# State-space stage: TensorE accumulates the four products of the turned-back states in three of four units

## The reference, cut to what matters

```
def step(x, u_blk):
    bu = einsum('btgh,gph->btgp', u_blk, b_bar)          # complex
    bu = bu.at[:, 0].add(a_bar * x)
    _, xs = associative_scan(affine_compose, (a, bu))    # xs_t = a_bar xs_(t-1) + bu_t
    y = einsum('btgp,ghp->btgh', xs, c_mat).real
```

## Time and profile before

| | |
|---|---|
| time, median of 3 runs | 2393.43 us (2393.11 to 2394.8) |
| span of the profiled execution | 2391.8 us |
| TensorE busy | 2247.6 us (94%) |
| VectorE busy | 1480.2 us (62%) |
| ScalarE busy | 1084.7 us (45%) |
| granted TensorE clock, mean | 0.981 |

### The profile page before, as it was taken

One profiled execution on the slowest core, in us unless ns is written; L12 is line 12 of the kernel. 1 busy time (PEld: TensorE's weight loads), 2 busy tenths in 40 slices (PEclk: granted clock), 3 DMA queues, 4 the chain that ended last, 5 costly groups with the idle time before them and its releaser, 6 DMA issues.

```text
span 2391.8 us, 35981 instructions
## 1 busy us (share of the span) xinstructions
PE 2247.6 (94%) x15110; PEld 1802.5 (75%) x15110; DVE 1480.2 (62%) x2392; ACT 1084.7 (45%) x1834; POOL 127.0 (5%) x171
## 2 busy tenths in 40 slices
PE   7988899999999999988999989989999998769999
PEld 5755567888886777778999853357888887669999
DVE  6477547565557577866467235655566576995454
ACT  5455434232226466655456345644232334545453
POOL 0000000000000000000010011200200101000210
PEclk9999999999999999999999999999999999989999
DMA  8263453444435555434554223442443435633543
GB/s 298 73 234 113 180 211 122 154 150 142 153 138 193 163 177 169 159 132 146 177 185 143 93 71 123 159 175 87 160 153 130 159 115 195 228 127 134 212 177 124
DMA packets 180753, 372.50 MB, mean 156 GB/s; under 512 B 7664, under 2 KB 108272, under 8 KB 167280
## 3 DMA queue, kind: packets, MB, share of 16 engines
q1 hardware_dynamic: 180592, 370.21, 44.6%
HBM read 339.74 MB, written 30.44 MB: 155 GB/s over the span
## 4 chain that ended last, share of the span: by engine, by line
PE 77%; DVE 15%; ACT 5%; issue 2%; DMA 1%; SPq 1%; POOL 0%; DVEq 0%; ACTq 0%; POOLq 0%
PE ps L169 76%; DVE sb_R L200 7%; DVE sb_R L232 2%; ACT sb_R L252 1%; DVE sb_H L200 1%; PE ps L179 1%; DVE sb_R L229 1%; DVE sb_X L217 1%; SPq L263 1%; DVE sb_WP L200 1%; DMA sb_R<-mod_w 1%; ACT sb_R L258 1%; DVE sb_R L217 1%; ACT L245 0%; DVE sb_R L214 0%
## 5 line engine op out<-in xcount | busy, mean ns | idle before, releaser
L169 PE MATMUL ps<-sb_HP,sb_WP 128*128 128x512 f32 (+1 forms) x5808 | 1071.1, 345 | 11.8 <-DVE sb_HP L200 5.5
L169 PEld LDWEIGHTS ps<-sb_HP,sb_WP 128*128 128x128 f32 x5808 | 915.1, 190 | 151.6 <-issue 12.9
L200 DVE TENSOR_TENSOR sb_WP<-sb_slot,sb_WP 128x1024 fp32r<-128x1024 f32 x380 | 468.1, 1237 | 545.7 <-ACT sb_WP L258 545.0
L258 ACT ACTIVATE sb_WP<-sb_slot 128x1024 fp32r<-128x1024 f32 x380 | 399.3, 1057 | 702.9 <-PE ps L169 680.4
L169 PE MATMUL ps<-sb_XP,sb_WP 128*128 128x256 f32 (+1 forms) x2976 | 498.9, 330 | 0.6 <-DVE sb_R L200 0.4
L169 PEld LDWEIGHTS ps<-sb_XP,sb_WP 128*128 128x128 f32 x2976 | 446.4, 191 | 52.3 <-DVE sb_R L200 0.9
L200 DVE TENSOR_TENSOR sb_R<-sb_R 128x256 f32<-128x256 f32 (+4 forms) x379 | 185.4, 524 | 8.5 <-ACT sb_R L252 5.6
L169 PE MATMUL ps<-sb_R 128*32 128x64 f32 (+7 forms) x1768 | 152.8, 285 | 29.6 <-DVE sb_R L200 7.7
L169 PEld LDWEIGHTS ps<-sb_R 128*32 128x32 f32 (+3 forms) x1768 | 106.6, 151 | 66.7 <-issue 30.2
L252 ACT ACTIVATE sb_R<-ps 128x512 f32<-128x512 f32 (+1 forms) x208 | 99.9, 513 | 103.9 <-PE ps L169 99.4
L252 ACT ACTIVATE sb_R<-sb_R 128x512 f32<-128x512 f32 (+4 forms) x111 | 76.2, 689 | 79.5 <-DVE sb_R L200 78.1
(11 more groups left out here) (161 smaller groups left out, 1895.3 us busy)
## 6 DMA issues: line engine op xcount, KB each, us to landing
sb_slot<-mlp_w SPq DMA_DIRECT2D x32, 2048.0 KB, 7.9
sb_slot<-mod_w SPq DMA_DIRECT2D x12, 2048.0 KB, 7.5
sb_R<-ada_w SPq DMA_DIRECT2D x12, 2048.0 KB, 7.6
sb_slot<-ada_w SPq DMA_DIRECT2D x24, 1024.0 KB, 4.9
sb_slot<-ffn_w_gate SPq DMA_DIRECT2D x22, 1024.0 KB, 5.5
sb_slot<-ffn_w_up SPq DMA_DIRECT2D x22, 1024.0 KB, 8.0
sb_slot<-ffn_w_down SPq DMA_DIRECT2D x9, 2048.0 KB, 7.8
sb_slot<-odd_w_in SPq DMA_DIRECT2D x32, 512.0 KB, 7.6
```

What stands on the lines that cost most here:

```text
L169: return self.e.matmul(out, w, x, start=start, stop=stop, skip_group_check=True)
L200: return BLANK if self.e is None else self.e.tensor_tensor(out, a, b, op)
L258: return self.e.activation(out, a, ACT.Copy) if scale is None else self.e.activation(out, a, ACT.Copy, scale=scale)
```

## The change

In units 0, 1 and 2 VectorE no longer adds the products of the turning back. It writes four planes of 64 columns a row, two into the halves of each row of `Vi` and two into the halves of `Vr`: the product of the real parts, minus the product of the imaginary parts (one `scalar_tensor_tensor`), and the two mixed products. They can't all be written at once, since the sources lie in `Vr` and `T1`: the first half of `Vr` overlaps the source in one column, so that the third product waits for the two before it, and the fourth for the third. TensorE runs each output matmul once for each plane, so that the accumulation in PSUM makes the sums. Unit 3 stays as it was.

```
+    def halves(self, z):
+        return self.v3(z)[:, :, 0:64], self.v3(z)[:, :, 64:128]
...
+        if u < 3:
+            (re1, re2), (im1, im2) = self.halves(Vi), self.halves(Vr)
+            pr, pi, Zr, Zi = (self.read(z) for z in (pr, pi, Vr, T1))
+            e.mul(re1, pr, Zr).then_inc(*e.sig())
+            e.stt(re2, pi, -1.0, Zi, ALU.mult, ALU.mult).then_inc(*e.sig())
+            e.wait_ge()
+            e.mul(im1, pi, Zr).then_inc(*e.sig())
+            e.wait_ge()
+            e.mul(im2, pr, Zi).then_inc(*e.sig("scanned", u))
+            return
...
-        XX = [self.v3(self.V[u % 2][:, 1, :]), self.v3(self.V[u % 2][:, 0, :])]
+        parts = self.halves if u < 3 else lambda z: (self.read(z),)
+        XX = [(i, x) for i in range(2) for x in parts(self.V[u % 2][:, 1 - i, :])]
...
-                for i in range(2):
+                for n, (i, x) in enumerate(XX):
                     for j in range(4):
                         q = 4 * j + f
-                        m = e.mm(o[32 * j:32 * j + 32, s, :], self.CA[u // 3][i][s + 1][:, j, f, :], XX[i][:, q, 63:127], False, s == 3 and i == 1)
+                        m = e.mm(o[32 * j:32 * j + 32, s, :], self.CA[u // 3][i][s + 1][:, j, f, :], x[:, q, :], False, s == 3 and n == len(XX) - 1)
```

## The result

The changed kernel takes 2402.7 us in the median (2400.53 to 2405.6, four runs) against 2394.11 us (2393.11 to 2394.82, four runs): a ratio of 1.004, interval 1.0029 to 1.0052. It is slower by some 9 us; forecast were 2405.2 us. The profiled execution took 2405.6 us, its span 2403.8 us.

The account below looks back on a forecast made before the run. VectorE bounds the scans now; afterwards TensorE, with 11.3 us of slack, decides. 3X - 11.3 = 13.3 us, less 1.5 us at outputs 3, makes +11.8 us: span 2403.6 us, time 2405.2 us, range 2396 to 2414 us.

Parts of the forecast that it names:

- What bounds the kernel: Four scans: VectorE's chain runs without pause to the last sums; TensorE is a second chain with 11.3 us of slack.
- VectorE's part: Turning back in units 0 to 2: 7.0 us becomes 5.0 us, a gain of 2.0 us a unit (0.5 to 2.4).
- X: TensorE's added cost a unit, outputs 0 to 2, for 256 more records: 8.2 us, ends 6.4 to 11.0 us.
- Along the chain: Scans 2 and 3: VectorE waits for later inputs, 0.5 and 9.5 us late; outputs 3 start 13.3 us later.
- Outputs 3: Unit 3's output matmuls get cheaper by 1.5 us (0 to 3.3) at the full clock.
- The loads: CA of units 1 and 2 and matrices of unit 3 stay hidden, costed at nothing; otherwise 1.5 us a load.
- A: Rival in TensorE's outputs: extra instruction blocks come in time, X = 3.9 us; +0.9 us, 2394.3 us, no change; chance 0.11.
- B: Rival: TensorE's clock falls to 0.5 over much of outputs 0 to 2 and inputs behind; +21.7 us, 2415 us; chance 0.09.
- C: Rival: VectorE stays the bound throughout, outputs 3 start 6 us sooner, 2387 us; needs X under 1.8 us; chance 0.06.

Follow-up runs that it names:

- dve_alone: Changed kernel's VectorE products without sums in units 0 to 2, but TensorE reads one plane of two, 256 records a unit as before: 2385.87 us, ratio 0.9959 to before.
- pe_alone: Kernel before, VectorE keeping its sums, with each output matmul of units 0 to 2 issued twice on the same sums: 2403.37 us, ratio 1.0030.
- narrow: Changed kernel with the second plane's matmuls moving 8 columns and not 64, as many instructions: 2402.08 us, ratio 1.0026 to before.
- wide: Changed kernel's VectorE, but TensorE issues one matmul of 128 columns for two of 64, 256 records a unit as before: 2387.25 us, ratio 0.9969 to before.
- unit1: Kernel before with the change made in unit 1 alone: ratio 0.9996 to before.
- unit2: Kernel before with the change made in unit 2 alone: ratio 0.9994 to before.
- early: Kernel before, but in unit 3 the real sum comes first and is signalled by itself, and TensorE runs its 128 records first: ratio 0.9987 to before.

## Why the prediction was right

- **What bounds the kernel** held: TensorE's second chain with 11.3 us of slack, which dve_alone (ratio 0.9959) and pe_alone (1.0030) show from both sides.
- **VectorE's part**: 4.9 us a unit against the 5.0 us forecast. The new operation takes 1.22 us where I took 1.35 us; it costs hardly more than a product.
- **X, TensorE's part**: 8.2 us were taken. From the first to the last record, outputs 0, 1, 2 took 14.3, 14.7 and 12.0 us against 6.6, 7.6 and 5.3 us: X = 7.7, 7.1 and 6.7 us. That is 21.5 us over three units, 3.1 us under the 24.6 us forecast. Inputs 3 took 1.5 us more as well (12.6 against 11.1 us), with pauses of 0.45 and 2.74 us in place of one of 1.60 us. The prediction had that term at nothing, so it was luck that it brought half of the miss back: 23.0 us in all. The mis-sized term is X: two further blocks at the pitch of 3.47 us are 6.9 us. I had taken nearly the mean of three pauses of 1.26 to 3.56 us, two of them the first of their outputs, while the pauses between the further blocks are 0.5 to 2.0 us; that a first pause holds time in which the queue starts again is my reading and not shown.
- **Along the chain**: from outputs 0 to outputs 3 94.8 us against 82.7 us, +12.0 us, forecast 13.3. The waits of VectorE stand where they were put (scan 2 short, scan 3 over 9 us, then the ratios), and none of TensorE is left at outputs 3. The prediction looked only at the third product of scan 3; 7.49 us of the wait stand before the first two, which want the real plane of the same inputs. The end is the same: from 2058.17 us, recurrence 3 starts 77.5 us later, and 77.6 us were forecast (2134.7 - 2057.04).
- **Outputs 3**: 9.69 us became 8.32 us to the gated product, 1.4 us less against the 1.5 us forecast; a pause of 4.35 us stands where one of 2.86 us was.
- **The loads** stayed hidden: TensorE has no wait for a DMA in the stage.
- **A** (blocks in time) fell by the pauses, four in outputs 0 of the changed kernel: in this stage TensorE lost 29.3 us in 18 pauses. The Trainium skill, page "Runtime: NRT & Kernel Launch", section "Instruction fetch mechanics", says that crossing a block is mostly hidden; the trace doesn't agree with it here.
- **B** (the clock) did not decide. The granted clock fell for a time in outputs 0 and 1 and not in outputs 2 (windows of TensorE after: length, busy, granted clock, DMA share, GB/s):

```profile
2058.20:2072.40 14.20, 9.22 (x513) 0.89 0.07 28
2095.80:2110.50 14.70, 9.18 (x514) 0.88 0.33 132
2135.50:2147.50 12.00, 8.04 (x513) 1.00 0.01 4
```

  At 1.00 outputs 2 still cost 6.7 us more. narrow had 0.50 through outputs 1:

```profile
2093.50:2107.20 13.70, 10.48 (x372) 0.50 0.23 71
```

  and its length is that of the changed kernel within 0.3 us from either start. Nor was there more half clock after the change: from outputs 0 to 2150 us the grant was at 0.5 for 21 us before and 14 us after.
- **C** (VectorE's whole gain) is what dve_alone and wide show. It needed X under 1.8 us, and X was 7.

The time, 2402.7 us, is 2.5 us under the forecast. As a change it is +8.6 us by the medians and +9.6 us by the ratio, against +11.8 us forecast. The trace gives 1.3 us of that miss up to outputs 3, from the 1.6 us of TensorE's work. The rest can't be told from the scatter: the length from outputs 0 grew by 10.9 us and that from scan 0 by 7.7 us in the same two traces.

## What to carry to other kernels

Before work is moved to TensorE, count its instructions, not only its columns: here a block of 256 instructions (128 small f32 records) came every 3.47 us at best, so in a long stream records of under 27 ns (3.47 us / 128) cost what the supply costs, and twice the columns in the same number of instructions cost the kernel nothing (wide is as fast as dve_alone). Slack belongs to a place: with the same 256 records outputs 3 start 2.1 us sooner where nothing waited behind them (unit 2) and 0.2 us later ahead of inputs that a scan wanted (unit 1). That is one trace each, and the times can't tell the two apart. Take a length within a trace from the start of the chain that decides, and look at how far its start moves among kernels that are equal up to there. When an engine has waited long for the last result, split that result so that it can begin with the first half, and look at once at what the wait had hidden.

## What the runs showed of the hardware that I had not expected

- The pitch of the blocks: 3.47 us to the hundredth in most cases, in the changed kernel and in narrow, at busy times of 1.99 and 1.58 us. A packet of 16 KB in 3.47 us is 4.7 GB/s.
- The pitch has two parts that the trace shows. In outputs 0 to 2 of the changed kernel the packet starts 1.0 to 1.1 us after the block ahead of it has begun (1.5 and 1.6 us where the pitch is 3.75 and 4.02 us), and the first record of the new block runs 2.2 to 2.4 us after the packet's start. Neither part follows the busy time of the block, 1.99 to 2.93 us. Why a packet doesn't start sooner isn't shown.
- Half clock elsewhere goes with the whole time. Up to outputs 0 unit1 and unit2 have the same instructions, yet outputs 0 start at 2051.0 us of the span in the one and at 2061.2 us in the other. Up to their scan 0 the clock was granted at 0.5 for 41 us in unit1 and for 71 us in unit2; near 297 us of the span, for instance, it is none in unit1 and 10.2 us in unit2. That scatter is as large as the effects here. A length within the trace leaves it out, but not what comes between the two starts of such a length: for early the ratio is 0.9987 (-3.1 us), the length -0.1 us from outputs 0 and -1.6 us from scan 0.
- A scalar_tensor_tensor on 128x1024 takes 1.22 us, a product 1.23 us.
